# Attention's probability times value product with the values stationary and two query tiles in two column groups

## What is computed

```python
for each head h, for each tile of 128 queries:
    s = q_nope @ k_nope.T + q_rope @ k_rope.T      # 128 x 1024, contraction 64 + 32 = 96
    p = softmax(s * scale, axis=-1)                # 1024 keys
    o = p @ v                                      # 128 x 64
o -> (1024 positions, 8 heads * 64)                # then y_a = o_a @ w_o[:512]
```

## Time and profile before

| | |
|---|---|
| median of 3 runs | 4018.43 us (4017.99 to 4021.6) |
| the profiled execution: its own time / its span | 4019.79 us / 4018.0 us |
| TensorE busy | 3684.5 us, 92% of the span |
| VectorE / ScalarE / GpSimd busy | 1665.7 / 1059.8 / 240.7 us |
| scans with attention | 715 to 1614 us |
| scans alone, to their end | 1614 to about 1727 us |
| granted TensorE clock, mean | 0.958 of 2.4 GHz |

### The profile page before, as it was taken

One profiled execution on the slowest core, in us unless ns is written; L12 is line 12 of the kernel. 1 busy time (PEld: TensorE's weight loads), 2 busy tenths in 40 slices (PEclk: granted clock), 3 DMA queues, 4 the chain that ended last, 5 costly groups with the idle time before them and its releaser, 6 DMA issues.

```text
span 4018.0 us, 57814 instructions
## 1 busy us (share of the span) xinstructions
PE 3684.5 (92%) x25608; PEld 2745.6 (68%) x25608; DVE 1665.7 (41%) x2518; ACT 1059.8 (26%) x1704; POOL 240.7 (6%) x302
## 2 busy tenths in 40 slices
PE   7969989899999989879999999988989989999998
PEld 4434444677777777734778878877867768878876
DVE  2251143344444444464443453455245442244225
ACT  1222211333333333201321231233233221132124
POOL 0110012111111111120000000000000000000000
PEclk9989988899999999989999999999989999999999
DMA  2231123211111011133211221122300311122113
GB/s 107 58 118 36 37 99 126 90 49 36 33 51 49 23 36 36 60 129 123 84 42 47 59 93 53 47 95 91 96 27 27 110 53 48 53 79 74 52 58 100
DMA packets 89689, 269.61 MB, mean 67 GB/s; under 512 B 11408, under 2 KB 11936, under 8 KB 89312
## 3 DMA queue, kind: packets, MB, share of 16 engines
q1 hardware_dynamic: 78816, 230.26, 18.2%
q0 software_dynamic: 10624, 35.66, 2.5%
HBM read 219.73 MB, written 46.14 MB: 66 GB/s over the span
## 4 chain that ended last, share of the span: by engine, by line
PE 75%; DVE 10%; issue 8%; ACT 3%; DMA 2%; POOL 1%; SPq 1%; DVEq 0%; POOLq 0%; ACTq 0%
PE ps L333 70%; DVE X L342 3%; PE ps L336 3%; PE ps L332 2%; DVE AR L342 2%; DVE SM L353 1%; DVE OTB L342 1%; POOL AR L342 1%; DVE HL L342 0%; ACT HH L339 0%; DMA qk_d<-AR 0%; ACT W L1818 0%; ACT WS L339 0%; DMA oa_d<-OTB 0%; DVE SA L342 0%
## 5 line engine op out<-in xcount | busy, mean ns | idle before, releaser
L333 PE MATMUL ps<-HH,WS 128*128 128x512 f32 (+1 forms) x3232 | 1001.3, 391 | 0.0
L333 PEld LDWEIGHTS ps<-HH,WS 128*128 128x128 f32 (+1 forms) x3232 | 607.9, 188 | 129.5
L333 PE MATMUL ps<-HL,WS 128*128 128x512 f32 x1616 | 639.3, 396 | 10.1 <-DVE HL L342 10.1
L333 PE MATMUL ps<-HT,W 128*128 128x512 f32 (+2 forms) x2048 | 590.4, 446 | 21.8 <-DMA W<-in_w_rw 21.8
L342 DVE TENSOR_TENSOR WS<-W,WS 128x1024 fp32r<-128x1024 f32 (+1 forms) x245 | 299.6, 1223 | 640.8 <-ACT WS L339 640.4
L333 PE MATMUL ps<-WS,SA 128*128 128x512 f32 x2112 | 493.4, 394 | 42.2 <-DVE SA L342 42.2
L333 PEld LDWEIGHTS ps<-HT,W 128*128 128x128 f32 (+1 forms) x2048 | 318.4, 194 | 277.5 <-issue 272.0
L339 ACT ACTIVATE WS<-W 128x1024 fp32r<-128x1024 f32 (+1 forms) x245 | 257.6, 1051 | 905.5 <-PE ps L333 893.5
L333 PEld LDWEIGHTS ps<-WS,SA 128*128 128x128 f32 x2112 | 399.3, 190 | 133.5 <-DVE SA L342 29.7
L333 PEld LDWEIGHTS ps<-HL,WS 128*128 128x128 f32 x1616 | 304.0, 188 | 75.5 <-issue 10.5
L333 PE MATMUL ps<-AR 64*64 64x64 f32 (+3 forms) x6544 | 299.7, 236 | 7.4 <-ACT AR L339 3.5
(11 more groups left out here) (251 smaller groups left out, 3480.6 us busy)
## 6 DMA issues: line engine op xcount, KB each, us to landing
W<-in_w_fd SPq DMA_DIRECT2D x88, 512.0 KB, 3.5
W<-in_w_fg SPq DMA_DIRECT2D x44, 512.0 KB, 3.5
W<-in_w_fu SPq DMA_DIRECT2D x44, 512.0 KB, 3.6
AR<-rw_d SPq DMA_DIRECT2D x80, 256.0 KB, 4.0
W<-in_w_tok SPq DMA_DIRECT2D x24, 512.0 KB, 3.6
rw_d<-X POOLq DMA_DIRECT2D x40, 256.0 KB, 3.4
X<-in_x SPq DMA_DIRECT2D x16, 512.0 KB, 7.9
W<-in_w_g SPq DMA_DIRECT2D x16, 512.0 KB, 3.7
```

Source lines behind the costliest of these rows:

```text
L333: return pe.e.matmul(o, l, r, start=start, stop=stop)
```

## The change

The product now has the values as stationary operand (64 columns) and the transposed probabilities as moving operand (128 columns), so its result is already transposed: 64 rows (value dimensions) by 128 queries. Two tiles are done at once: the products of the first write PSUM partitions 0 to 63, those of the second partitions 64 to 127, alternating. Since the result has the queries along its columns, the division by the row sum moves ahead of the transposes: VectorE takes the reciprocal in T(i), scales the 128 x 1024 exponentials in place with it, and TensorE's T(i) waits for that. P(m) serves tiles 2m and 2m+1 and comes after T(2m+1); the two tiles of a pair are query tiles q and q+4 of the head. ScalarE copies the 128 x 128 result to `AOT`. The transposes of the output, VectorE's copies of them and `AOP` are gone. The output goes to `oa_d` once a head in two DMAs. `APT` gets two more buffers, taken from free room of the two scans (in EX and W).

```diff
+        AOT = [OTB, HT[:, 7168:7680]]
+        def apt(i):
+            return (W1[:, 0:1024], W1[:, 1024:2048], SC[0].spare, SC[1].spare)[i % 4]
+        def head_tile(i):
+            return i // 8, i % 8 // 2 + 4 * (i % 2)
 
         def att_steps(scores, transp, pv, load):
             load(0)
             yield
             for i in range(66):
-                if i % 8 == 2 and i // 8 + 1 < 8:
+                if i % 8 == 4 and i // 8 + 1 < 8:
                     load(i // 8 + 1)
                 if i < 64:
                     scores(i)
                     yield
                 if 1 <= i <= 64:
                     transp(i - 1)
                     yield
-                if i >= 2:
-                    pv(i - 2)
+                if i % 2 and i >= 3:
+                    pv((i - 3) // 2)
                     yield
...
 @@ att_pe @@
             def transp(i):
                 for g in range(2):
                     b = take(pe, "pT", i, g)
-                    pe.wait_ge(*at("ae_att", "p", i))
+                    pe.wait_ge(*at("ve_att", "p", i))
...
-            def pv(i):
-                h, q = divmod(i, 8)
-                b = take(pe, "pv", i)
-                pe.wait_ge(*at("ae_att", "pT", i, 1))
+            def pv(m):
+                h = m // 4
+                b = take(pe, "pv", m)
+                pe.wait_ge(*at("ae_att", "pT", 2 * m + 1, 1))
                 for j in range(8):
-                    x = mm(pe, ps[:, b, 0:64], APT[i % 2][:, j * P:(j + 1) * P], AVH[h % 2][:, j, :], j == 0, j == 7)
-                x.then_inc(*pe.sig("pe_att", "pv", i))
-                if i % 16 == 15:
-                    for g in range(2):
-                        b = take(pe, "oT", i, g)
-                        pe.wait_ge(*at("ve_att", "o", i))
-                        for j in range(4):
-                            x = tr(pe, ps[:, b, j * P:(j + 1) * P], AOP[:, (4 * g + j) * P:(4 * g + j + 1) * P])
-                        x.then_inc(*pe.sig("pe_att", "oT", i, g))
+                    for y, cols_ in enumerate(ROWS):
+                        x = mm(pe, ps[cols_, b, 0:P], AVH[h % 2][:, j, :], apt(2 * m + y)[:, j * P:(j + 1) * P], j == 0, j == 7)
+                x.then_inc(*pe.sig("pe_att", "pv", m))
...
@@ att_ve @@
-            def pv(i):
-                h, q = divmod(i, 8)
+            def transp(i):
                 rs = sm(272 + i % 4, 1)
                 ve.wait_ge(*at("ae_att", "p", i))
                 ve.e.reciprocal(rs, rs).then_inc(*ve.sig("ve_att", "inv", i))
                 ve.wait_ge(*at("ve_att", "inv", i))
-                ve.wait_ge(*at("pe_att", "pv", i))
...
+                ts(ve, APB[i % 2], APB[i % 2], rs, None, ALU.mult, None).then_inc(*ve.sig("ve_att", "p", i))
-            return att_steps(scores, skip, pv, skip)
+            return att_steps(scores, transp, skip, skip)
...
@@ att_ae @@
+            def pv(m):
+                h, q = divmod(m, 4)
+                ae.wait_ge(*at("pe_att", "pv", m))
+                if h >= 2:
+                    ae.wait_ge(*at(f"dma_oa{h % 2}", h - 2, 1))
+                cp(ae, AOT[h % 2][:, q * P:(q + 1) * P], ps[:, bank("pv", m), 0:P]).then_inc(
+                    *ae.sig("ae_att", "o", m, frees=("pv", m)))
+            return att_steps(scores, transp, pv, skip)
```

More of the change, by code:

```diff
@@ L906, in program @@
         APB = [HT[:, 5120 + 1024 * i:6144 + 1024 * i] for i in range(2)]
-        AOP, AOP3 = HT[:, 7168:8192], v3(HT[:, 7168:8192], 8)
-        APT = [W1[:, 1024 * i:1024 * (i + 1)] for i in range(2)]
+        AOT = [OTB, HT[:, 7168:7680]]
[3 more added lines that the diff above has]
+            return i // 8, i % 8 // 2 + 4 * (i % 2)
         def att_steps(scores, transp, pv, load):
@@ L934, in load @@
                 if h >= 2:
-                    sp.wait_ge(*at("pe_att", "pv", 8 * (h - 2) + 7))
+                    sp.wait_ge(*at("pe_att", "pv", 4 * (h - 2) + 3))
                 sp.e.dma_start(AQT[x], a["qk_d"][h, 0]).then_inc(*dma(f"dma_head{x}", h, "q"))
@@ L942, in scores @@
             def scores(i):
-                h, q = divmod(i, 8)
+                h, q = head_tile(i)
                 b = take(pe, "sc", i, n=2)
@@ L1018, in transp, with pv @@
                     ae.wait_ge(*at("pe_att", "pT", i, g))
-                    if i >= 2:
-                        ae.wait_ge(*at("pe_att", "pv", i - 2))
-                    cp(ae, APT[i % 2][:, 512 * g:512 * g + 512], ps[:, bank("pT", i, g), :]).then_inc(
+                    if i >= 4:
+                        ae.wait_ge(*at("pe_att", "pv", i // 2 - 2))
+                    cp(ae, apt(i)[:, 512 * g:512 * g + 512], ps[:, bank("pT", i, g), :]).then_inc(
                         *ae.sig("ae_att", "pT", i, g, frees=("pT", i, g)))
-            return att_steps(scores, transp, skip, skip)
-        def att_ge(ge):
[L1026 to L1031, removed]
+            def pv(m):
[6 more added lines that the diff above has]
+            return att_steps(scores, transp, pv, skip)
+        def att_ge(ge):
+            def pv(m):
+                if m % 4 == 3:
+                    h = m // 4
+                    ge.wait_ge(*at("ae_att", "o", m))
+                    for g, half_ in enumerate(ROWS):
+                        ge.e.dma_start(oa_d[64 * h:64 * h + 64, 512 * g:512 * g + 512], AOT[h % 2][half_, :]).then_inc(
+                            *dma(f"dma_oa{h % 2}", h, g))
             return att_steps(skip, skip, pv, skip)
@@ L1070, in scan_memory @@
             c.TT, c.Y, c.U = heads(512), heads(256), heads(256)
-            c.SS, c.OB = v3(part(256), 4), part(512)
+            c.SS, c.OB, c.spare = v3(part(256), 4), part(512), part(1024)
             c.TC = cst["TCF"] if d == 0 else cst["TCB"]
@@ L1492, in outa_sp @@
                 sp.wait_ge(*end("att", g))
-            sp.wait_ge(*at("dma_oa", 63, 1))
+            sp.wait_ge(*at("dma_oa0", 6, 1))
+            sp.wait_ge(*at("dma_oa1", 7, 1))
             sp.e.dma_start(OAT3, oa_d.rearrange("(k p) n -> p k n", p=P)).then_inc(*dma("dma_oat", 0))
```

## The result

The changed kernel takes **4080.8 us** (median of four runs, 4077.2 to 4091.0) against 4018.2 us (4017.7 to 4021.6) for the kernel before, run on the same chip: a ratio of 1.0158, interval 1.0139 to 1.0178. It is 62.6 us slower. The forecast was 4091 us, 73 more than before, with a chance of 0.85 for slower. The profiled execution of the changed kernel was the longest of its four: 4090.97 us, 71.2 us over the profiled one of before.

What follows compares the result with a forecast made beforehand. TensorE was taken to bound the stretch of attention with scans, so its work and waits both add time. Terms -57 - 8 + 98 + 5 + 35 = +73 us on 4019.8 gave 4092.8, median 4091 us; range 4028 to 4165.

Steps and rivals of the forecast that it cites:

- The product: TensorE's P in attention: 118 us before, 61 us after in pairs of tiles, so 57 us less.
- The base case: P's two column groups run at once on TensorE, so a pair of tiles takes 1.9 us.
- the rival without it: P's column groups don't run at once: no 57 us gain, 4148 us, or 4119 with weight load exposed; chance 0.07.
- The output's transposes: 32 transposes after P go, 3.5 us, with the waits around them, 2.3 and 1.9 us: 8 us less.
- The new wait: TensorE's T waits for VectorE's scaling, mean 1.65 us over 64 tiles, 105 us; 98 more after 7 off at iteration starts.
- The rival of overlapping waits: New waits absorb the 53 us TensorE already waits at iteration starts: 4010 us, if under 0.94 us a tile; chance 0.14.
- ScalarE: Its 32 copies of P's result, under 0.4 us each, hide in idle time: cost nothing, 13 us if uncovered.
- The rounds: Attention takes 161 rounds, leaving 70 instead of 38 scan rounds alone with longer start waits: 5 us more (0 to 10).
- The clock: Half of the 27 new waits over 2 us drop TensorE to 1.2 GHz, 3 us each: 35 us more (0 to 117).
- the rival in which every wait sends it down: TensorE's clock falls at nearly every new wait, costing 117 us: 4173 us; chance 0.12.
- the four signs named beforehand: T's wait 85 to 120 us; P pair 1.9 us; scaling 0.75 to 0.9 us; joint stretch 875 us, clock about 0.88.

Runs made afterwards that it cites:

- experiment 5: experiment 1 with both tiles' products in one column group, output rows 0 to 63, ScalarE copying in two pieces: 4014.8 us, ratio 0.9987 to the kernel before.
- experiments 6: experiment 1 with an empty attention step where the old P stood, so attention spreads over 193 rounds instead of 161: 3955.5 us, ratio 0.9837 to before.
- experiment 8: The kernel before, old product and output transposes kept, with the scaling added early on VectorE, ahead of the next tile's row maximum: 4030.5 us, ratio 1.0023.
- experiment 10: The changed kernel with only an empty attention step added, so attention spreads over 193 rounds: 4063.3 us, ratio 1.0107 to the kernel before.
- experiments 3: The kernel before with the scaling in T's place on VectorE and T waiting for it, old product kept: 4160.0 us, ratio 1.0347.
- experiment 1: The changed kernel with VectorE's reciprocal and scaling moved one round earlier, to S(i+1)'s place ahead of the row maximum: 3970.8 us, ratio 0.9871 to before.
- experiment 11: The changed kernel with the PSUM bank ring turned by six after the scans, so later code starts at before's bank: 4073.7 us, ratio 1.0131 to before.
- the filler: The changed kernel with one unused 512-column product of constants on TensorE ahead of T's wait: 4043.6 us, ratio 1.0057 to the kernel before.

## Why the prediction was right, and where its terms were off

The sign and the mechanism held: T waits for the scaling, the wait costs more than the product gains, and the clock adds to it. The size held too, 73 us forecast, 71 in the profiled executions, 63 in the medians, but that it came so close is partly luck, as the sum at the end shows. Term by term:

- **The product, -57 forecast, -67 found.** All P blocks take 131.6 us before and 64.8 after. After was right (1.90 us a pair where 1.9 was said). Before was mis-sized: 1.85 us a tile came from one block at 2.4 GHz, the mean of all 64, some of them at the low clock, is 2.06. The base case, that two column groups run at once, was right, and the rival without it is refuted by experiment 5. The Trainium skill ("TensorE: Matmul & The Clock Gate", part 3) says that a weight load overlaps running products only where the row group differs. The trace does not agree with this rule: two groups with all 128 rows in common start 0.01 us apart, and even within one group a load and 128 moving columns take 0.11 us together. The same part also names a second way, a load into a background weight buffer; whether that is what happens here no run shows.
- **The output's transposes, -8 forecast.** They and their waits are gone; with P 75 us by experiments 6 and 8, where 65 was said for both.
- **The new wait, +105 in total forecast, 112 found**, 58 waits of 1.93 us. The lags read tile by tile in the trace of before carried the forecast. What it takes off the older waits was put too low: I took 7 us off for the starts, and 16 us are gone there (63.6 to 47.3 over both scans; 15 and 19 in experiments 10 and 3). That TensorE's stop lets VectorE catch up before the start's own wait would explain it; no experiment tested that. Another 16 us are gone from small waits of other kinds. All of TensorE's waits up to the output projection are 108.9 us before and 184.6 after; without the new wait, and without the 4 us at the output's transposes, 16 us of the difference are left beside the starts. So the net is 80, not 98. The rival of overlapping waits was right for about a quarter of the old start waits, and 80 us are 1.25 us a tile, over the 0.94 that would have decided. ScalarE, put at nothing, costs nothing that shows: no P waits for its copies in the joint stretch.
- **The rounds, +5 forecast, +6** by experiments 1 and 6 in the traces up to the end of the scans. With the wait in place it is more, 17 us between the traces of the change and experiment 10, or 9 if experiment 11, the same program up to there, stands for the change.
- **The clock, +35 forecast, +37** by the filler and +37 by TensorE's busy time in experiment 1. With 58 waits the clock went down only 18 times more than before, so the rival in which every wait sends it down, 117 us, is refuted.
- **Behind the scans, 0 forecast, +19** in the profiled executions, 7 in the medians. Nothing in the forecast looked at which bank the unchanged code begins with. This term had no line of its own.

Up to the end of the scans the sum of what was found is -67 - 8 + 112 - 16 - 16 + 6 + 37 = +48 us; the traces show +52, and the terms, some of which share a few us, are no more exact than that. Two errors of the forecast, 10 us too small a gain and 18 us too large a net wait, make 28 us too much cost; 3 us of other terms and the 4 us not accounted for leave 21, and the unforeseen 19 us behind the scans came close to cancelling them. That was luck. Of the four signs named beforehand, the wait's total and the length of P came as said; the scaling measured 0.80 us within 0.75 to 0.9; the joint stretch is 857 us at a clock of 0.90 (0.88 said). For it 875 us were said, where 161 rounds of 3.1 us are 499 and not 495; the sum as it stood gives 880.

## What to carry to other kernels

Two column groups with 64 stationary columns each run at once and halve a product whose result is only 64 wide; with the output's transposes gone, that part of the change is worth 75 us, and 44 of them need the two groups. But it forced a step on another engine (the division) from behind the product to in front of it. In a program whose engines each follow a fixed order, a cross-engine step that is put into the same round as its user costs its own length plus the lag of that engine, each time; one round earlier it costs little, here 9 us in experiment 8. The lag can be read from the trace before the change is made, tile by tile, and short stops of TensorE cost more than their length: here 37 us of clock on 112 us of waits.

## What was not expected of the hardware

- More work made the kernel faster: one 512-column product of constants in front of each wait gave 37 us, and brought the granted clock of the joint stretch from 0.90 to 0.96.
- The same 9216 TensorE records behind the scans take 2286 to 2306 us, depending on the kernel in front of them, and 2286 to 2290 where they begin at the same PSUM bank as before. Each is from one trace; the medians do not tell it apart from chance.
- Nearly the same waits, 104 us, add 50 us to TensorE's busy time with the old product (experiments 3 and 8) and 34 with the new one (experiments 10 and 6). Why is open; the blocks of P have little part in it.
